# First attention of a two-block transformer kernel: scores of seven of eight pairs of heads from split keys and queries

## The reference, cut to what matters

```
qkv = einsum('bsd,de->bse', h, w_qkv)          # h: 256 x 1024, 16 heads of 64
s = einsum('bqhd,bkhd->bhqk', q_c, k_band) * 64 ** -0.5 + bias[h]   # chunks of 64 queries
s = where(key_pos >= 0, s, -1e30)              # own chunk and the 8 before it
p = softmax(s);  o = einsum('bhqk,bkhd->bqhd', p, v_band)
out = einsum('bsd,de->bse', o, w_o)
```

## Time and profile before

| | us |
|---|---|
| median of three runs | 978.15 |
| lowest and highest | 977.05, 978.16 |
| profiled execution | 977.05 |
| its span, first to last instruction | 975.7 |
| PE busy | 969.4 (99%) |
| DVE busy | 680.5 (70%) |
| ACT busy | 588.9 (60%) |
| POOL busy | 66.2 (7%) |

### The profile page before, as it was taken

The page is one execution under the profiler, slowest core; times in us unless marked ns, Lnnn a source line. Parts: engine busy times, 40 slices in busy tenths (PEclk is TensorE's granted clock), DMA queues, the critical chain, the costliest instruction groups (busy, mean ns, idle before and its releaser), DMA issues.

```text
span 975.7 us, 13395 instructions
## 1 busy us (share of the span) xinstructions
PE 969.4 (99%) x5146; PEld 826.6 (85%) x5146; DVE 680.5 (70%) x1161; ACT 588.9 (60%) x1042; POOL 66.2 (7%) x80
## 2 busy tenths in 40 slices
PE   9999999999999999999999999999999999999997
PEld 7887888888888898888888888888888888988886
DVE  5887776666667889666666688778767554877564
ACT  6777755454456897645454466547876555684443
POOL 1323110000000242000000000000011000000000
PEclk9999999999999999999999999999999999999999
DMA  9853445555555435545555556445543544335551
GB/s 372 311 191 130 173 173 203 208 189 199 178 209 175 156 147 208 181 173 201 209 187 202 178 209 242 164 175 189 197 167 105 195 145 169 133 132 209 177 189 44
DMA packets 27120, 180.33 MB, mean 185 GB/s; under 512 B 2993, under 2 KB 3889, under 8 KB 6321
## 3 DMA queue, kind: packets, MB, share of 16 engines
q1 hardware_dynamic: 26336, 176.98, 50.5%
q0 software_dynamic: 288, 2.10, 0.6%
q10 hardware_dynamic: 432, 0.39, 0.1%
HBM read 178.41 MB, written 1.05 MB: 184 GB/s over the span
## 4 chain that ended last, share of the span: by engine, by line
PE 99%; DVE 0%; ACT 0%; POOL 0%; issue 0%; DVEq 0%; POOLq 0%
PE bank L338 26%; PE bank L293 16%; PE bank L295 16%; PE bank L294 16%; PE bank L346 13%; PE bank L308 1%; PE bank L468 1%; PE bank L484 1%; PE bank L589 1%; PE bank L518 1%; PE bank L309 1%; PE bank L529 1%; PE bank L460 1%; PE bank L378 0%; PE bank L381 0%; PE bank L496 0%
## 5 line engine op out<-in xcount | busy, mean ns | idle before, releaser
L1342 DVE TENSOR_TENSOR lo<-raw,hi 128x1024 fp32r<-128x1024 f32 x318 | 375.7, 1228 | 20.1 <-ACT hi L815 19.9
L815 ACT ACTIVATE hi<-raw 128x1024 fp32r<-128x1024 f32 x318 | 320.2, 1050 | 100.1 <-PE bank L295 98.2
L338 PE MATMUL bank<-X,hi 128*128 128x512 f32 x1016 | 266.9, 395 | 0.0
L338 PEld LDWEIGHTS bank<-X,hi 128*128 128x128 f32 x1016 | 185.0, 189 | 33.0
L346 PEld LDWEIGHTS bank<-X,lo 128*128 128x128 f32 x1016 | 138.6, 190 | 10.1
L346 PE MATMUL bank<-X,lo 128*128 128x256 f32 x1016 | 141.6, 282 | 0.0
L846 ACT ACTIVATE bt<-bank 128x256 f32<-128x256 f32 x135 | 51.0, 380 | 141.2 <-PE bank L338 132.9
L1356 DVE TENSOR_TENSOR zr<-bank,bt 128x256 f32<-128x256 f32 x64 | 27.1, 424 | 109.0 <-ACT bt L846 109.0
L293 PE MATMUL bank<-hi,zh 128*128 128x512 f32 x256 | 100.0, 390 | 0.0
L295 PE MATMUL bank<-hi,zl 128*128 128x512 f32 x256 | 99.8, 390 | 0.0
L294 PE MATMUL bank<-lo,zh 128*128 128x512 f32 x256 | 99.6, 389 | 0.0
(11 more groups left out here) (347 smaller groups left out, 1422.7 us busy)
## 6 DMA issues: line engine op xcount, KB each, us to landing
raw<-in_w SPq DMA_DIRECT2D x64, 1024.0 KB, 4.7
raw<-in_rin SPq DMA_DIRECT2D x8, 1024.0 KB, 4.7
raw<-in_wk SPq DMA_DIRECT2D x4, 1024.0 KB, 10.5
raw<-in_wq SPq DMA_DIRECT2D x4, 1024.0 KB, 8.5
raw<-in_wo SPq DMA_DIRECT2D x4, 1024.0 KB, 4.7
raw<-in_mk SPq DMA_DIRECT2D x4, 1024.0 KB, 4.8
raw<-in_mv SPq DMA_DIRECT2D x4, 1024.0 KB, 4.7
raw<-in_rout SPq DMA_DIRECT2D x4, 1024.0 KB, 4.7
```

The source lines that it names most:

```text
L338: return PE.matmul(bank[b][:, :], wh[:, c:c + P], x[:, k_, :, :].rearrange("p a b -> p (a b)"), start=k_ == 0, stop=k_ == NC - 1, skip_gro ...
L815: ACTE.activation(hi[u_ % HIS][:, c], raw[u_ % RAW][:, c], ACT.Copy).then_inc(hi_cut, 1)
L1342: DVE.tensor_tensor(lo[u_ % RAW][:, c], raw[u_ % RAW][:, c], hi[u_ % HIS][:, c].bitcast(F32), ALU.subtract).then_inc(lo_cut, 1)
```

## The change

The scores of pair 0 are made as before (`first_scores`). For pairs 1 to 7 four new buffers in slot 3, two pairs deep, hold high and low parts of `k` and `q`. ScalarE copies the high parts (`pair_highs(j+1)`, at the end of step j behind the exponential of the odd head), VectorE subtracts the low parts (`pair_lows(j+1)`, at the end of step j behind `soft` of the odd head). PE's `pair_scores` waits for the low parts (`kq_low`) instead of for POOL's scaling, and makes each of its four products by three float32r matmuls. From pair 3 on the new writers wait until the scores that used the same buffer are done.

```diff
+    kh, kl, qh, ql = [slot(n, 3, [2, S], F32R, off=2048 * i) for i, n in enumerate(("kh", "kl", "qh", "ql"))]
...
+        def first_scores():
...
         def pair_scores(j):
-            p.wait_ge(kq_scaled, 4 * (j // 2) + 2 + j % 2)
-            if j == 0:
-                p.wait_ge(q_scaled, 1)
+            p.wait_ge(kq_low, 2 * j)
             done = [fill(("s", 2 * j + e), (4, 6)[e]) for e in range(2)]
             for a, b, n, c in ((P, S, S, 0), (0, P, P, 256)):
-                for e in range(2):
-                    r = slice(64 * e, 64 * e + 64)
-                    m = PE.matmul(bank[(4, 6)[e]][:, c:c + n], q[r, j, a:b], k[r, j, 0:n], start=True, stop=True, skip_group_check=True)
-                    if c:
-                        m.then_inc(done[e], 1)
+                for i, (q_, k_) in enumerate(((qh, kh), (qh, kl), (ql, kh))):
+                    for e in range(2):
+                        r = slice(64 * e, 64 * e + 64)
+                        m = PE.matmul(bank[(4, 6)[e]][:, c:c + n], q_[r, j % 2, a:b], k_[r, j % 2, 0:n], start=i == 0, stop=i == 2,
+                                      skip_group_check=True)
+                        if c and i == 2:
+                            m.then_inc(done[e], 1)
...
-            if j < 8:
+            if j == 0:
+                first_scores()
+            elif j < 8:
                 pair_scores(j)
...
+        def pair_highs(j):
+            a.wait_ge(kq_scaled, 4 * (j // 2) + 2 + j % 2)
+            a.wait_ge(x_low, low_at("mix0", NC - 1))
+            if j > 2:
+                a.wait_ge(*full["s", 2 * j - 4])
+                a.wait_ge(*full["s", 2 * j - 3])
+            ACTE.activation(kh[:, j % 2, :], k[:, j, :], ACT.Copy).then_inc(kq_high, 1)
+            ACTE.activation(qh[:, j % 2, :], q[:, j, :], ACT.Copy).then_inc(kq_high, 1)
...
                     soft(n, TT)
+                if e and j < 7:
+                    pair_highs(j + 1)
...
+        def pair_lows(j):
+            if j > 2:
+                d.wait_ge(*full["s", 2 * j - 4])
+                d.wait_ge(*full["s", 2 * j - 3])
+            for n, (x_, h_, l_) in enumerate(((k, kh, kl), (q, qh, ql))):
+                d.wait_ge(kq_high, 2 * j - 1 + n)
+                DVE.tensor_tensor(l_[:, j % 2, :], x_[:, j, :], h_[:, j % 2, :].bitcast(F32), ALU.subtract).then_inc(kq_low, 1)
...
                 if j < 8:
                     soft(i, TT)
+                if e and j < 7:
+                    pair_lows(j + 1)
```

More of the change, by code:

```diff
@@ L131, in build @@
     zx_made, ox_gated, ox_high, ox_low = sem("zx_made"), sem("ox_gated"), sem("ox_high"), sem("ox_low")
+    kq_high, kq_low = sem("kq_high"), sem("kq_low")
     f_high, f_low, res_made = sem("f_high"), sem("f_low"), sem("res_made")
@@ L508, in pe @@
             p.wait_ge(*free["wv", b])
-        def pair_scores(j):
-            p.wait_ge(kq_scaled, 4 * (j // 2) + 2 + j % 2)
-            if j == 0:
-                p.wait_ge(q_scaled, 1)
-            done = [fill(("s", 2 * j + e), (4, 6)[e]) for e in range(2)]
+        def first_scores():
+            p.wait_ge(kq_scaled, 2)
+            p.wait_ge(q_scaled, 1)
+            done = [fill(("s", e), (4, 6)[e]) for e in range(2)]
             for a, b, n, c in ((P, S, S, 0), (0, P, P, 256)):
@@ L517, in pair_scores @@
                     r = slice(64 * e, 64 * e + 64)
-                    m = PE.matmul(bank[(4, 6)[e]][:, c:c + n], q[r, j, a:b], k[r, j, 0:n], start=True, stop=True, skip_group_check=True)
+                    m = PE.matmul(bank[(4, 6)[e]][:, c:c + n], q[r, 0, a:b], k[r, 0, 0:n], start=True, stop=True, skip_group_check=True)
                     if c:
                         m.then_inc(done[e], 1)
+        def pair_scores(j):
+            p.wait_ge(kq_low, 2 * j)
+            done = [fill(("s", 2 * j + e), (4, 6)[e]) for e in range(2)]
+            for a, b, n, c in ((P, S, S, 0), (0, P, P, 256)):
+                for i, (q_, k_) in enumerate(((qh, kh), (qh, kl), (ql, kh))):
[5 more added lines that the diff above has]
+                            m.then_inc(done[e], 1)
         def pair_av(j):
```

## The result

| | before | after |
|---|---|---|
| median of six runs each, us | 978.17 | 982.53 |
| lowest and highest | 977.05, 978.25 | 981.69, 983.58 |
| profiled execution, its span | 977.05, 975.7 | 983.17, 981.9 |

What follows compares the result with a forecast made beforehand. PE was taken to bound the kernel, its chain 99% PE. Waits of 3.6 us plus 0.5 for the score block made +4.1 on 978.15, so 982.2 us, with a range of 980.0 to 985.6.

Steps and rivals of the forecast that it cites:

- Part 4: PE's scores of the next pair wait for VectorE's low parts: seven steps late by 0.15 to 1.12 us, together 3.6.
- Step j=5: Wait before scores of pair 6: 0.72 us, plus 0.3 if subtractions stretch 1.43 times beside POOL's adds.
- Step j=6: Wait before scores of pair 7: 1.12 us; freer scaling -0.5 and a hit second subtraction +0.2 cancel the previous step's 0.3.
- The clock: PE's granted clock, 2.4 GHz: holes charged nothing; a microsecond at 1.2 GHz behind each would cost 0.5 us each.
- Part 1: PE's score block: float32r matmuls 0.71 us against 0.64 for f32, +0.07 a pair, +0.5 over seven pairs.
- Parts 2 and 3: ScalarE's high-part copies cost nothing; VectorE's two low-part subtractions, 0.42 us each, end 0.76 behind its softmax work on the pair.
- A: Rival: 128 float32r columns stream slowly in PE's score block, block 1.04 us, total +6.4, 984.6 us; chance 0.22.
- B: Rival: float32r row halves run one after the other in PE's score block, total +9.1, 987.3 us; chance 0.07.
- C: Rival: weight loads hidden, 128 columns cost their stream, score block -0.16 us a pair, total +2.5, 980.7 us; chance 0.13.
- D: Rival: low parts ready before PE's scores, so not slower; 977.0 us with C's block; chance 0.07.
- E: Rival: added VectorE and ScalarE work, 4.9 us, makes these engines the step's bound; no chance of its own.
- F(j)+0.80-S(j+1): Lateness of PE's next scores: VectorE's end of pair j, plus 0.80 us for subtractions and hand-over, less the scores' old start.

Runs made afterwards that it cites:

- e1: Changed kernel with the high and low parts of pair j+1 made earlier in the same step, ahead of each head's exponential or reciprocal; 978.23 us, ratio 1.0006.
- e2: Changed kernel with its high and low parts and PE's waits kept, but scores made from plain f32 q and k; 982.41 us, ratio 1.0048.
- g2: f3 with its three 128-column float32r products issued three times over, 42 more pairs of matmuls; 982.36 us.
- f3: Changed kernel with both the early high and low parts and POOL's adds held back; 977.74 us, ratio 0.9994.
- e3: Changed kernel with POOL's seven adds of squares on 1 column instead of 256, leaving out the norm of mem; 979.75 us, ratio 1.0020.
- f2: Changed kernel with POOL's seven adds held back to places where VectorE reads PSUM, nothing left out; 979.67 us, ratio 1.0014.
- f1: The changed kernel run again unaltered, for a second trace; 982.12 us, ratio 1.0039.
- f4: Changed kernel with pair 1 also from plain f32 q and k, high and low parts from pair 2 on; 981.63 us, ratio 1.0034.
- e4: Changed kernel with seven idle 512-column matmuls put ahead of PE's low-part wait for pair 6, the bank's wait now first; 982.60 us, ratio 1.0053.

## Why the prediction was right, and where its terms were wrong

- **Part 4, the wait, was the cause.** Five steps came as worked out: 0.96 forecast and 0.97 measured for j=0, 0.24 against 0.23 and 0.22, 0.15 against 0.14 twice. e1 and e2 show the cause from both sides: without the waits and with the new matmuls the loss is 0.5 us, with the waits and without the matmuls it is all there. From step 1 on the measured figures hold a score block that is 0.03 shorter, so the waits proper are 0.24 to 0.25 and 0.16 to 0.17 (the scores start 1.04 and 0.97 behind `pair_av` instead of 0.80).
- **Step j=5 was mis-sized.** I took 0.72 and let a stretch by the factor 1.43 add 0.3. The rows do not bear a factor. Each operation beside an add became longer by about the same amount: the `lo` cut by 1.75-1.22 = 0.53, a subtraction by 0.94-0.42 = 0.52, two scalings together by 1.11-0.55 = 0.56. On an operation of 0.42 us that is much more than 1.43 times. So 0.72 + 2 x 0.52 = 1.76, and 1.77 was measured. The trace of before could have said so, since its `lo` cut (88.94 to 90.69) ran beside POOL's adds from end to end:

```profile
87.95 3.35 POOL L1981 TENSOR_TENSOR sq<-sq,sq 128x256 f32<-128x256 f32 x3
```

- **Step j=6 went as argued, in part.** The scalings ran free (0.55). The second subtraction was not hit (0.42 at 102.64); POOL's add fell on the `lo` cut behind it. e2 shows 0.64 (8.72-8.08) where I had 1.12-0.5+0.2 = 0.82. But "the two cancel" failed, since step 5's side was 1.04 and not 0.3. With e2's step 6, which has no fall of the clock, the steps are late by 0.97+0.23+0.14+0.22+0.14+1.77+0.64 = 4.1 us. Five blocks that are 0.03 shorter are in this, so the waits alone are some 4.3, not 3.6.
- **The clock: charged nothing, wrong.** In both traces of the changed kernel it fell behind the hole of 1.72 us. That cost 0.83 us beside e2, and 0.47 to 0.83 beside all three traces that kept the clock.
- **Part 1, the block: +0.07 forecast, -0.03 measured** (59.98-59.15 = 0.83 against 0.86). I set every pair at 0.119. The starts of the pairs are 0.22, 0.12, 0.12, 0.05 and 0.12 apart, and the turn follows 0.20 behind the last. My price gave 0.93: the 0.10 too much are one distance of 0.05 for 0.12, once a block, and 0.03 at the end. The 0.05 stands where the matmuls go from 256 to 128 columns: the loads keep their 0.11 to 0.12, the first narrow matmul still starts 0.12 behind its load (59.49, 59.61), as the wide ones do, and the second only 0.05 behind its own (59.61, 59.66). So seven blocks give -0.2, not +0.5. The conclusion stood: PE gains next to nothing.
- **Parts 2 and 3 held.** ScalarE's `qh` is done at 66.48 where `ql` starts at 66.90; the subtractions take 0.42 with 0.34 between starts.
- **The sum.** Forecast +4.1. Measured +4.36 in the medians, and 4.1 (with e2's step 6) to 4.9 (with the fall) in the traces. That the sum came so close is luck in its parts: the block was too large by 0.7 and the waits were too small by 0.7, and the 0.3 that is left in the medians is less than one fall of the clock, which was not in the sum. The mechanism that decided the sign and most of the size was not luck.
- **The rivals.** A (narrow pairs at 0.227) and B (the row halves one after the other) fell by the trace, whose block is 0.83. C had the sign of the block's change but neither its size (-0.03 and not -0.16) nor its mechanism: g2 has 0.107 to 0.110 a pair and not 0.053. D fell by the waits in the trace and by e2. E, the added work as such, fell by e1.

On the block the Trainium skill (TensorE: Matmul & The Clock Gate, "Back-to-back issue gap") gives 134 cycles, 0.056 us, for 128 columns in its table of the isolated gap. The trace agrees in one place of each block, 59.61 to 59.66. In a sequence with a load for each matmul g2 decides: 0.107 to 0.110.

## What to carry to other kernels

When work is put ahead of a consumer, find where its producer ends in the profile of before and subtract: F(j)+0.80-S(j+1) gave five of seven stalls to 0.02 us, on an engine that was only 70% busy. It failed in the step where another engine ran beside the new work, so look there for rows of the same kind of operation, and ask whether they grew by a factor or by an amount. In this kernel two operations behind the longest chain cost their length less the room that was there; put into gaps ahead of a wait, the same operations cost 0.5 us in place of 4.4 (e1), and nothing that can be measured once POOL's adds were moved too (f3). Replacing a two-pass f32 matmul by three one-pass matmuls gained PE 0.03 us on a block of 0.86, with weight loads that start 0.11 us apart.

## What the runs showed of the hardware

- POOL's add of two SBUF tiles makes VectorE's operation beside it longer by about half a microsecond: 0.94 us instead of 0.42 for a subtraction of two SBUF tiles, 1.11 instead of 0.55 for two scalings, 1.75 instead of 1.22 for a cut of 1024 columns. With the adds on one column (e3) or elsewhere (f2) the subtractions are back at 0.42. Each of the three adds in step 5 begins beside another of these operations (90.87, 91.74, 92.67 beside those of 90.83, 91.87 and 92.73), as if each waited once for one add; no run tests that. Operations that read PSUM are not touched (0.41 for L1475 at 90.61 in the trace of before, beside an add), nor are ScalarE's copies (0.40). The Trainium skill (VectorE: DVE Perf Modes, "Two Vector instructions with no wait between them") says that an operation with two SBUF inputs, or one in a 2-port mode, reads through a second SBUF read interface that is shared with GpSimd. That section of the Trainium skill gives no time for it. The trace agrees for the operations with two SBUF inputs, which are longer beside POOL; it does not show in which mode the scalings ran.
- A hole of 1.72 us in PE's work (2.0 in its weight loads) came before a fall of the granted clock to its lower level in two traces (the changed kernel's and f1) and left it alone in two others (e2 with 1.74, f4 with 1.72). Where it fell, the first slow matmuls start 0.8 us (94.56) and 1.7 us (94.87 in f1) after PE had resumed, and the slow ones end at 97.8 and 98.3. What decides between the two cases is open.
- 128-column float32r matmuls with a weight load each follow at 0.107 to 0.110 us a pair of row halves (g2), 256-column ones at 0.12.
- Two waits of PE in the other order cost 0.09 us a step (e4). This is unexplained.
